# Starting the second block inside the last feed-forward, and its recurrence among the gate tiles, in a two-block float32 kernel

## What is computed

```python
def first_block(x, ...):                       # two layers
    for l in range(2):
        x = x + 0.5 * swiglu_ffn(rmsnorm(x, norm_ffn1[l]), ...)
        x = x + hybrid_mixer(rmsnorm(x, norm_mix[l]), ...)
        x = x + 0.5 * swiglu_ffn(rmsnorm(x, norm_ffn2[l]), ...)
    return rmsnorm(x, final_norm)

def second_block(x, c, ctx, c_ctx, ...):
    # i = 0: a recurrent mixer on x and on a context
    h  = rms_norm(x,  norm_g[0]) * (1 + scale)   + shift      # scale, shift from silu(c) @ ada_w
    hc = rms_norm(xc, norm_g[0]) * (1 + scale_c) + shift_c
    #   proj = h @ rw_in: r, k, v, low-rank inputs lw, la (token-shift mixed), and a gate g
    #   w = decay(tanh(lw) @ w2), a = sigmoid(la @ a2), kk = normalised key, per head
    #   S_t = S w_t - (S kk_t)(kk_t a_t)^T + v_t k_t^T, forwards and backwards, ctx then x
    #   y = (groupnorm(o) + bonus) * silu(g);  x = x + gate * (y @ rw_out), the same for ctx
    # i = 1: differential attention of x over [ctx, x], 8 heads, then x = x + gate * y
    return x
```

## Time and profile before

| | |
|---|---|
| median of 3 runs | 2594.71 us (2594.16 to 2594.93) |
| the profiled execution | 2599.11 us, its span from first to last instruction 2597.2 us |
| TensorE busy | 2510.1 us, 97% |
| DVE, POOL, ACT busy | 897.3, 666.5, 545.1 us |
| granted TensorE clock, mean | 0.989 |
| chain that ended last | PE 87%, DVE 7%, ACT 3% |

### The profile page before, as it was taken

One profiled execution on the slowest core, in us unless ns is written; L12 is line 12 of the kernel. 1 busy time (PEld: TensorE's weight loads), 2 busy tenths in 40 slices (PEclk: granted clock), 3 DMA queues, 4 the chain that ended last, 5 costly groups with the idle time before them and its releaser, 6 DMA issues.

```text
span 2597.2 us, 49707 instructions
## 1 busy us (share of the span) xinstructions
PE 2510.1 (97%) x20866; PEld 2000.5 (77%) x20866; DVE 897.3 (35%) x1776; ACT 545.1 (21%) x1211; POOL 666.5 (26%) x609
## 2 busy tenths in 40 slices
PE   8999999999999999999999799969999999999999
PEld 7888888888878888888888345448888888655558
DVE  2210564112012114641120522135555555236642
ACT  2001030100110010301000111124555554222331
POOL 6442005514404420065230000023444444000000
PEclk9999999999999999999999899979999999999999
DMA  6444444444444444445443321200000000212112
GB/s 259 170 173 168 157 151 178 171 154 179 179 149 166 177 163 158 146 178 178 154 154 114 132 78 65 81 1 3 3 3 3 4 3 19 83 42 89 65 49 82
DMA packets 45693, 291.03 MB, mean 112 GB/s; under 512 B 5376, under 2 KB 7568, under 8 KB 13728
## 3 DMA queue, kind: packets, MB, share of 16 engines
q1 hardware_dynamic: 38304, 261.24, 27.8%
q0 software_dynamic: 7168, 26.60, 3.0%
HBM read 286.77 MB, written 1.05 MB: 111 GB/s over the span
## 4 chain that ended last, share of the span: by engine, by line
PE 87%; DVE 7%; ACT 3%; issue 1%; DMA 0%; SPq 0%; DVEq 0%; ACTq 0%
PE psum L542 61%; PE psum L558 5%; PE psum L1003 3%; PE psum L992 3%; PE psum L1005 2%; DVE arena L1912 1%; PE psum L952 1%; PE psum L810 1%; PE psum L1089 1%; PE psum L1036 1%; PE psum L980 1%; PE psum L939 1%; PE psum L1229 1%; PE psum L823 1%; PE psum L1013 1%
## 5 line engine op out<-in xcount | busy, mean ns | idle before, releaser
L542 PE MATMUL psum<-arena,ring 128*128 128x256 f32 (+1 forms) x7264 | 1728.3, 398 | 24.2 <-ACT arena L1380 10.3
L542 PEld LDWEIGHTS psum<-arena,ring 128*128 128x128 f32 x7264 | 1373.5, 189 | 360.0 <-issue 159.5
L1748 POOL TENSOR_TENSOR arena<-arena 128x1024 f32<-128x1024 f32 (+2 forms) x288 | 376.6, 1307 | 820.8 <-DVE arena L1853 789.9
L1003 PE MATMUL psum<-arena 64*64 64x64 f32 x2560 | 160.0, 225 | 3.3 <-DVE arena L2077 3.2
L1401 ACT ACTIVATE arena<-arena 128x256 f32<-128x256 f32 x88 | 36.7, 417 | 549.0 <-DVE arena L1861 549.0
L1003 PEld LDWEIGHTS psum<-arena 64*64 64x64 f32 x2560 | 139.4, 134 | 15.6 <-issue 8.5
L558 PE MATMUL psum<-arena,ring 128*128 128x512 f32 (+1 forms) x320 | 131.2, 554 | 10.3 <-ACT arena L1693 8.9
L1005 PE MATMUL psum<-arena 64*64 64x64 f32 x2048 | 133.4, 219 | 0.0
L1862 DVE TENSOR_TENSOR arena<-psum,arena 128x256 f32<-128x256 f32 x88 | 37.4, 425 | 257.3 <-PE psum L542 257.3
L734 POOL TENSOR_TENSOR ring<-arena,ring 128x512 f32<-128x512 f32 x8 | 11.1, 1393 | 447.6 <-ACT arena L1485 447.6
L992 PE MATMUL psum<-arena 64*64 64x64 f32 x2560 | 114.3, 222 | 9.4 <-DVE arena L2071 4.3
(11 more groups left out here) (272 smaller groups left out, 2357.5 us busy)
## 6 DMA issues: line engine op xcount, KB each, us to landing
ring<-in_weights SPq DMA_DIRECT2D x245, 1024.0 KB, 4.8
arena<-in_ada POOLq DMA_DIRECT2D x48, 512.0 KB, 4.0
arena<-in_const POOLq DMA_DIRECT2D x1, 1312.0 KB, 10.2
arena<-in_x SPq DMA_DIRECT2D x1, 1024.0 KB, 4.9
arena<-in_ctx SPq DMA_DIRECT2D x8, 128.0 KB, 2.8
arena<-in_lora SPq DMA_DIRECT2D x1, 1024.0 KB, 7.8
out<-arena SPq DMA_DIRECT2D x8, 128.0 KB, 4.6
arena<-in_p SPq DMA_DIRECT2D x1, 102.0 KB, 4.7
```

What stands on the lines that cost most here:

```text
L542: mm = self.nc.tensor.matmul(out, self.ring[:, slot % RING, i * P:(i + 1) * P], rhs, start=(kc == 0), stop=(kc == len(moving) - 1))
L1003: mm = mm_(ps_xy[b][halves[h], 1, u, :], t_, y_, start=True, stop=True)
L1748: tt(dst, a_, b_, ALU.add if n else ALU.mult).then_inc(s.mod_product, 1)
```

## The change

1. *Into the last feed-forward.* Context and low-rank weights are loaded by POOL's queue as soon as the last layer's mixer output is added. POOL sums the context's squares; TensorE makes their mean with one matmul after down-product 4 of every ffn2 (also in the first layer, where the result is not used); POOL and ACT make the context half of h2. The bank order of the eight down-products is permuted so that stage A's first tiles find their banks empty without the last one.
2. *Two norms in one root.* ACT squares x with the square root of (final_gain^2 + eps) as scale; one mean, one root and one reciprocal give h2's x half directly (`x_gain`). The final norm of x itself is made later, by POOL, behind product 2. The first two products (the low-rank inputs) are made by halves: context columns first, the x mean among them, then x columns.
3. *Stage A's weights* start at ring place 2, right behind the last used slot but one, and the stages are no longer padded. Of the loads, 17 and 24 remain of 20 and 25. Stage A's tiles use four banks (0, 1, 2, 5), the early scan tiles a side lane (6, 7).
4. *The recurrence among the gate tiles.* Pair 0's work waits for partial release of the ring (26 products for `v_rev` and `prod`, 30 for `bk` and `ar`); its low-rank, key-norm, first-gram and inverse steps are put between gate products 24 to 31. `bk` and `ar` of one pair now share two slots.
5. *Attention.* The value tiles get bank 7 alone, all others of stage B use seven banks.

The core of the diff:

```diff
-SECOND_A_SLOTS, SECOND_B_SLOTS = slots_of(SECOND_A_TILES), slots_of(SECOND_B_TILES)
+SECOND_A_SLOTS, SECOND_B_SLOTS = SECOND_A_TILES // SLOT_TILES, SECOND_B_TILES // SLOT_TILES
+SECOND_A_FROM = 2
+def part_left(ring_slot):
+    return RING + LOADS_BEFORE_A + ring_slot - SECOND_A_FROM + 1
+FIRST_PAIR_PARTS_LEFT = part_left(SECOND_A_FROM + SECOND_A_SLOTS - 3)
+LAST_PART_LEFT = part_left(SECOND_A_FROM + SECOND_A_SLOTS - 5)
...
 def second_a_order():
-    o = Order(FIRST)
-    o.add(("final", "mean_square"), "act")
-    o.add(("rw", "mean_square"), "act")
+    o = Order(FIRST, main=(0, 1, 2, 5), side=(6, 7))
+    o.add(("x", "mean_square"), "act")
...
 def second_b_order():
-    o = Order(SCAN, banks=RW_OUT_BANKS)
+    o = Order(SCAN, main=(2, 3, 4, 5, 0, 1, 6), values=(7,))
...
-            o.add(("v", i // 2 + 1), "act")
+            o.add(("v", i // 2 + 1), "act", "values")
...
         # SyncE
-            sp.wait_ge(s.bank_full, FIRST.full(("ffn2", "down", DC - 1), LAYERS - 1))
-            for m in range(DC):
-                sp.dma_start(xx[:, m, 0:T], ctx_in[:, m, :]).then_inc(s.context_loaded, 16)
-            sp.dma_start(lora_w, lora_in).then_inc(s.context_loaded, 16)
+            for i in range(SECOND_A_SLOTS):
+                r, before = (SECOND_A_FROM + i) % RING, LOADS_BEFORE_A + i
+                was = before - RING if i >= RING else LOADS_BEFORE_A - RING + r
+                sp.wait_ge(s.slot_used, RING + was + 1)
+                sp.dma_start(ring[:, r, :], weights[before]).then_inc(s.slot_landed[r], 16)
...
         # TensorE, in the first block
+                        if ffn == "ffn2" and m == CONTEXT_AFTER:
+                            pe.wait_ge(s.ctx_summed, lay + 1)
+                            nc.tensor.matmul(st.bank(("context", "mean_square")), mean_of_d, ctx_sum, start=True,
+                                             stop=True).then_inc(s.bank_full, 1)
...
         # TensorE, stage A
-            st.all_banks_empty(SECOND_A)
-            mean_square(("final", "mean_square"), LAYERS * NRES * DC)
-            bank = st.bank(("rw", "mean_square"), T2)
-            for kc in range(DC):
-                pe.wait_ge(s.sq_ready, kc + 1)
-                mm = nc.tensor.matmul(bank, mean_of_d, sq2[:, kc, :], start=(kc == 0), stop=(kc == DC - 1))
+            for c in range(2):
+                st.k = at
+                for i in range(2):
+                    for kc in range(DC):
+                        if i == 0:
+                            pe.wait_ge(s.h_ready, c * DC + kc + 1)
...
+                        if c == 0 and i == 0 and kc == 3:
+                            after_down(3)
+                            out_ = st.bank(("x", "mean_square"))
+                            for m in range(DC):
+                                pe.wait_ge(s.x_squared, LAYERS * NRES * DC + m + 1)
+                                mm = nc.tensor.matmul(out_, mean_of_d, x_squares[:, m, :], start=(m == 0), stop=(m == DC - 1))
...
         # TensorE, end of stage A
-            for q in range(FIRST_Q, 0):
-                side(q, "middle")
-                side(q, "end")
+            rw_in(3 * DC)
+            pe.wait_ge(s.lora_in, 4)
+            pe.wait_ge(s.lora_loaded, 16)
+            for kind in ("w", "a"):
+                for d in range(2):
+                    low_rank(st.bank((kind, 0, d), T2), kind, 0, d).then_inc(s.bank_full, 1)
+            rw_in(3 * DC + 1)
+            pe.wait_ge(s.kk_inverse, 1)
+            spread(st.bank(("kk_norm", 0), T2), kk_root[:, 0, :, :]).then_inc(s.bank_full, 1)
+            for m in range(3 * DC + 2, 3 * DC + 6):
+                rw_in(m)
             first_gram(0)
-            for level in (1, 2):
-                lower_product(0, level)
-                next_inverse(0, level)
+            rw_in(4 * DC - 2)
+            lower_product(0, 1)
+            for kc in range(DC):
+                if kc == DC // 2:
+                    next_inverse(0, 1)
+                mm = st.piece(last_gate, h2[:, kc, :], kc == 0, kc == DC - 1)
+            mm.then_inc(s.bank_full, 1)
+            lower_product(0, 2)
+            st.finish(SECOND_A_FROM + SECOND_A_SLOTS)
+            first_gram(1)
+            next_inverse(0, 2)
...
         # ScalarE
+            for m in range(6):
+                square_x(m)
+            for m in range(DC):
+                act.wait_ge(s.ctx_scaled, m + 1)
+                shift_h(m, 0)
+            for m in range(6, DC):
+                square_x(m)
...
         # direction(n, d), on DVE or GpSimd
+        eng.wait_ge(s.slot_used, RING_AT_REST if n else FIRST_PAIR_PARTS_LEFT)
...
         # GpSimd
+            pool.wait_ge(s.dve_taken, FIRST.taken(("w_out", DC - 1), last))
+            pool.dma_start(xx[:, :, 0:T], ctx_in).then_inc(s.context_loaded, 16)
+            pool.dma_start(lora_w, lora_in).then_inc(s.lora_loaded, 16)
+            square_sum(ctx_sum, xx[:, :, 0:T], ctx_squares).then_inc(s.ctx_summed, 1)
...
+            pool.wait_ge(s.dve_taken, FIRST.taken(("ffn2", "down", DC - 1), last))
+            square_sum(x_sum, x, ctx_squares).then_inc(s.x_summed, 1)
+            pool.wait_ge(s.x_inverse, 1)
+            for m in range(DC):
+                link(ts(xx[:, m, T:], x[:, m, :], final_gain[:, m:m + 1], None, ALU.mult))
+                tt(xx[:, m, T:], xx[:, m, T:], rms, ALU.mult).then_inc(s.x_moved, 1)
...
         # VectorE
-            link(nc.vector.reciprocal(rstd, rms))
+            link(nc.vector.reciprocal(rstd, rstd))
             for m in range(DC):
-                stt(xx[:, m, T:], x[:, m, :], final_gain[:, m:m + 1], rstd, ALU.mult, ALU.mult).then_inc(s.x_normed, 1)
+                stt(h2[:, m, T:], x[:, m, :], x_gain[:, m:m + 1], rstd, ALU.mult, ALU.mult).then_inc(s.h_scaled, 1)
...
             begin_inverse(0)
-            for level in (1, 2):
-                mask_lower(0, level)
+            mask_lower(0, 1)
+            mask_lower(0, 2)
+            begin_inverse(1)
```

More of the change, by code:

```diff
@@ L255, in first_order @@
     feed_forward("ffn2")
+    first = o.lane_place[("ffn2", "down", 0)][1]
+    for i, bank in enumerate((3, 1, 2, 0, 5, 4, 6, 7)):
+        o.banks["main"][(first + i) % BANKS] = bank
     return o.close()
@@ L787, in _ @@
                 else:
[L788 to L793 removed]
+                    sp.wait_ge(s.slot_used, RING + LOADS_BEFORE_B + i - RING + 1)
@@ L1760, in _ @@
+            pool.wait_ge(s.mixed, 3 * DC + 2)
+            pool.wait_ge(s.dve_taken, SECOND_A.taken(("kk_norm", 0)))
+            direction(0, 0, pool, tt, ts, link, tmp)
+            pool.wait_ge(s.first_backward_ready, 1)
+            bonus_input(0)
+            for q in range((PAIRS + 1) * GROUPS):
                 pair, g = divmod(q, GROUPS)
@@ L1869, in feed_forward @@
                         take(stt(x[:, m, :], full(name), 0.5, x[:, m, :], ALU.mult, ALU.add), name, wait=False)
+                        if ffn == "ffn2" and m == CONTEXT_AFTER:
+                            dve.wait_ge(s.act_taken, FIRST.taken(("context", "mean_square"), lay))
+                            nc.vector.reciprocal(rms, rms).then_inc(s.ctx_inverse, 1)
                 feed_forward("ffn1", 0)
```

378 lines of the change are left out of this document (234 added, 144 removed).

## The result

| | before | after |
|---|---|---|
| median of 4 runs each | 2594.64 us (2594.16 to 2594.93) | 2536.57 us (2535.33 to 2537.15) |
| ratio | | 0.9777, 95% interval 0.9764 to 0.979 |
| profiled execution, its span | 2599.11 us, 2597.2 us | 2537.01 us, 2535.3 us |
| TensorE busy, granted clock | 2510.1 us (97%), 0.989 | 2492.3 us (98%), 0.998 |

The change gains 58.1 us between the medians and 61.9 us between the profiled spans. The forecast was 62.5.

The account below looks back on a forecast made before the run. TensorE, 97% busy, was taken to bound the kernel. Gains of 26.4 (second block's start), 27.2 (recurrence's start) and 8.9 us (attention), 62.5 in sum, came off the 2594.7 us median: 2532.2 us, range 2528 to 2545.

Parts of the forecast that it names:

- part C: Start of the recurrence: pair 0's work among gate products shortens 92.6 us to 65.4, a gain of 27.2 us.
- part D: Attention: a bank of its own for value tiles removes six TensorE waits for ACT's exponential, a gain of 8.9 us.
- Part A: Step into the second block: TensorE's 47.2 us stretch shrinks to 18.7 us plus a 2.1 us stall, gaining 26.4 us.
- T0 to C: From the last down-product's end (T0) to ACT's copy of the second low-rank product (C): about 19.5 us forecast.
- The rule for SP's issue: First stage A weights are issued when 8 tiles of the last down-product remain, 2.8 us before its end.
- Part B: Stage A's 26 mixed products: four banks instead of eight and the final norm on POOL change nothing, either way.
- E: End of the last mixed product, from which the recurrence's start is counted; turn 0's third level was forecast 65.4 us later.
- The first (clock): TensorE's stand for the first weights lets the clock fall: 3.0 us lost, 2535 us, chance 0.22.
- second (POOL): POOL's sum of x squares blocks DVE's scalings: 2 to 4 us lost, 2535 to 2536 us, chance 0.08.
- The third: Pair 0 comes late again, so the first gram waits for `direction`: about 2541 us, chance 0.1.
- The fourth, fifth and sixth: Value bank only moves the wait: 2541 us, chance 0.06; overlap absent: 2558, 0.03; four banks slow stage A: 2627, 0.02.

## Why the prediction was right, and where not

**The time.** 2532.2 was forecast, 2536.57 measured, inside 2528 to 2545. The sum of parts came out almost exactly: 62.5 us forecast between the spans, 61.9 found; a span of 2534.7 forecast, 2535.3 found. That it is so close is partly luck: part C gave 2.0 us less and the scan took 2.0 more, while part D gave 1.9 more and 1.2 us came from the clock behind the key products' stand (16.89 us before, 15.74 after), which the change doesn't touch. The error in the time is in the last step, which took the same 62.5 us off the median. The 4.4 us by which the profiled execution of before stood above its median was carried over as if it were still there to be had. The changed kernel's profile stands 0.4 us above its median. Repetition put the profile of before in an upper group of its executions. Its key products ran 2.9 us longer than at full clock; that this is 2.9 of the 4.4 us is likely but not shown, since no execution of the lower group has a trace. Where the other 1.5 us lie is open.

**Part A, right.** T0 to C: 19.5 forecast, 19.40 found. The +0.6 us up to T0 can't be told from scatter, since T0 lay between 1429.0 and 1432.4 us in the profiled executions. With the means elsewhere (+0.6 and +0.5, forecast 1.3 in all) the part gave 26.7 us for 26.4. Parts C and D were undone one by one; part A was not, and its worth is read from this stretch. The rule for SP's issue gave T0 - 2.8; the trace has it at 1427.31, which is T0 - 3.0. The stand is 1.84 us (2.1 forecast). The context sum was through at 1337.85, 63 us before TensorE used it.

**Part B, right.** The mixed products took 172.24 and 172.70 us, with the final mean of 0.44 among them. Four banks didn't show.

**Part C, right in mechanism, 2.0 us too large.** The term that was too small is the new stretch: 65.4 forecast, 67.13 found. `direction` began at E + 33.5 (32.7 forecast). DVE's ended at E + 43.3, POOL's, for which the gram waits too, at E + 44.5 (43.6), 1.8 us before the gram (2.0). Gate 30 ended at E + 54.4 (53.5). Of the 1.7 us too many, 0.6 lie in the second pair of low-rank tiles, 1.70 us where 1.13 was counted; the rest is spread over the joints: 0.1 us where TensorE goes from one kind of product to another. From gate 30's end to the third level it took 1689.54 - 1676.82 = 12.7 us for 11.9; the stretch of the kernel before was 92.4 and not 92.6.

**Not forecast: the scan, 2.0 us longer.** The prediction placed the extra table loads beside gate products. One of them is instead the first exponential of turn 1, in front of a copy on the path, and cost 1.1 us to 1.3, as its removal showed. The 0.5 us stand put down to "issue" comes and goes. The remaining few tenths are unexplained.

**Part D, right in mechanism, 1.9 us too small.** The 8.9 us were taken from the list of waits. Each wait cost 1.75 us and not 1.49, six times 0.26 = 1.6 us more; undoing the part alone brought 10.7 us back in the stretch. No wait for the probabilities took its place.

**The rivals.** The first (clock) and second (POOL) exist, and both were avoided narrowly: with a stand of 5.06 us instead of 1.84 the first costs 2.9 us, and POOL's sum missed the scalings by 1 us. The price of 4.7 us for POOL's first instruction isn't twice the 1.90 us of the earlier trace rows; it took 3.60. The third was missed by 1.8 us. The fourth, fifth and sixth left no trace.

## What to carry to other kernels

Sum a gain between profiled spans, and before taking it off a median ask whether the profiled execution of before is a typical one; the surplus of an untypical one is not gained. A listed idle isn't all that a wait costs: here each of six cost 0.26 us more, in overlap of matmuls lost and a slower start. Where a step is moved on ACT, look for the table load that moves with it, and where it lands among the copies that TensorE waits for.

## What the hardware showed that was not expected

- The same stand of 3.25 to 3.35 us before the same 64 records was followed by 14.05 us at a granted clock of 1.00 in some profiled executions and 17.06 us at 0.82 in others. Behind 1.84 us nothing was lost, behind 5.06 us 2.9 us.
- A 256-column scaling on DVE that met one of POOL's instructions ended 0.3 us after that instruction's end, four times out of four, whether POOL's took 3.60 or 0.79 us; alone it is listed with 0.47 us.
- 1.49 us of listed wait before a 512-column product stretched the period by 1.75 us.
